# Stacked decoder blocks on one core: the expert weights of the second mixture dealt to the partitions in eights

## The reference, cut to what matters

```python
# t: 256 tokens x 1024 features; comb: 256 x 16 weights, non-zero in one group per token
a = silu(einsum('td,edf->tef', t, w_gate)) * einsum('td,edf->tef', t, w_up)   # w_gate, w_up: 16 x 1024 x 256
y = einsum('tef,efd->td', a * comb[:, :, None], w_down)                       # w_down: 16 x 256 x 1024
```

## Time and profile before

| what | us |
|---|---|
| median of 3 runs | 2881.32 |
| lowest and highest of them | 2875.06, 2892.28 |
| the profiled execution, its own time | 2874.71 |
| span of its instructions | 2872.9 |
| layer 0 of the second mixture, about | 2108 to 2298 |
| layer 1 of the second mixture, about | 2671 to 2853 |

### The profile page before, as it was taken

The page is one execution under the profiler, slowest core; times in us unless marked ns, Lnnn a source line. Parts: engine busy times, 40 slices in busy tenths (PEclk is TensorE's granted clock), DMA queues, the critical chain, the costliest instruction groups (busy, mean ns, idle before and its releaser), DMA issues. The chain is left out here.

```text
span 2872.9 us, 35384 instructions
## 1 busy us (share of the span) xinstructions
PE 2539.0 (88%) x15219; PEld 1502.3 (52%) x15219; DVE 794.5 (28%) x1806; ACT 410.5 (14%) x926; POOL 53.7 (2%) x67
## 2 busy tenths in 40 slices
PE   2889899998989999999997878689689977998997
PEld 2776788785773333333333323265554466656543
DVE  1211221288221122221212000124434413373122
ACT  1102000001121111011110000113211101352111
POOL 0000000070000000000000000000000000000000
PEclk9999999998989999999999999898879988697899
DMA  8333255642009999999999999932139962301481
GB/s 268 117 109 126 73 191 205 209 143 74 1 31 392 393 385 385 379 373 393 371 393 393 393 394 393 391 108 88 53 120 371 374 122 80 117 1 63 159 300 56
DMA packets 328586, 645.33 MB, mean 225 GB/s; under 512 B 12875, under 2 KB 98017, under 8 KB 328417
## 3 DMA queue, kind: packets, MB, share of 16 engines
q1 hardware_dynamic: 318608, 636.51, 61.4%
q10 hardware_dynamic: 9809, 6.41, 0.8%
HBM read 641.84 MB, written 1.05 MB: 224 GB/s over the span
## 5 line engine op out<-in xcount | busy, mean ns | idle before, releaser
L1330 PE MATMUL bank<-ring,xn 128*32 128x512 f32 x4896 | 564.3, 596 | 7.9 <-DMA ring<-od_moe_gu 6.2
L1142 PE MATMUL bank<-xn,ring 128*128 128x256 f32 x2048 | 462.9, 390 | 54.2 <-DVE xn L2878 17.7
L1142 PEld LDWEIGHTS bank<-xn,ring 128*128 128x128 f32 x2048 | 401.1, 196 | 116.6 <-issue 41.1
L1330 PEld LDWEIGHTS bank<-ring,xn 128*32 128x32 f32 x4896 | 157.1, 110 | 362.3 <-issue 349.0
L1395 PE MATMUL bank<-ring,att 128*32 128x512 f32 x2448 | 276.7, 593 | 1.3 <-ACT att L1961 1.3
L1295 PE MATMUL bank<-ring,xn 128*64 128x512 f32 x336 | 170.8, 658 | 64.9 <-issue 64.9
L2406 DVE TENSOR_TENSOR sq<-att,bank 32x512 f32<-32x512 f32 x70 | 48.0, 686 | 507.8 <-ACT att L1972 342.4
L1297 PE MATMUL bank<-ring,xn 128*64 128x512 f32 x336 | 171.2, 659 | 0.0
L1395 PEld LDWEIGHTS bank<-ring,att 128*32 128x32 f32 x2448 | 78.6, 110 | 171.9 <-issue 170.8
L1249 PE MATMUL bank<-xn,ring 128*128 128x256 f32 x704 | 153.6, 380 | 0.0
L1249 PEld LDWEIGHTS bank<-xn,ring 128*128 128x128 f32 x704 | 134.6, 191 | 18.7 <-issue 0.3
(11 more groups left out here) (265 smaller groups left out, 2324.0 us busy)
## 6 DMA issues: line engine op xcount, KB each, us to landing
ring<-od_moe_gu SPq DMA_DIRECT2D x112, 2048.0 KB, 17.3
ring<-od_moe_down SPq DMA_DIRECT2D x56, 2048.0 KB, 18.0
ring<-ada_w SPq DMA_DIRECT2D x24, 2048.0 KB, 15.1
ring<-moe_w_gate SPq DMA_DIRECT2D x32, 1024.0 KB, 9.2
ring<-moe_w_up SPq DMA_DIRECT2D x32, 1024.0 KB, 8.4
ring<-moe_w_down SPq DMA_DIRECT2D x16, 2048.0 KB, 13.8
ring<-ev_w_in SPq DMA_DIRECT2D x10, 2048.0 KB, 19.8
ring<-ev_ffn_gu SPq DMA_DIRECT2D x10, 2048.0 KB, 12.8
```

The costliest lines, as they stand in the source:

```text
L1142: mm = nc.tensor.matmul(ps[:, c * T:(c + 1) * T], kblk(b)[:, k, u * T + c * P:u * T + (c + 1) * P], x[:, k, :], start=k == 0, stop=k == KD ...
L1330: return nc.tensor.matmul(PSB[f.b][j * QP:(j + 1) * QP, :], src[:, k, at:at + QP], kblk(b)[:, k, :], start=k == 0, stop=k == KD - 1)
```

## The change

The 1024 feature rows of an expert's gate or up matrix are laid over the partitions in another way. Before, partition `p` got rows `p`, `p + 128`, `p + 256` and so on. Now it gets rows `8p` to `8p + 7`, which lie one behind the other in HBM, 8 KB in all. The place in SBUF is the same: eight pieces of 1 KB, 2 KB apart, because the two experts of a pair lie side by side in a slot. So that the tokens have their features in the same order, the gather for the second mixture takes as its stationary operand every eighth column of `xn_tok`, starting at `k`, in place of 128 neighbouring ones. The gather of the first mixture stays as it was. The number of loads, of matmuls and of all other instructions is unchanged. The load in the branch for more than 96 tokens and its gather are changed in the same way.

```diff
@@ experts
             def pair(W, n):
-                W = W[l].rearrange("e (k p) n -> e p k n", p=P)
+                W = W[l].rearrange("e (p k) n -> e p k n", p=P)
                 return [(lambda e, j: lambda b: (kblk(b)[:, :, j * E2_FF:(j + 1) * E2_FF], W[e]))(2 * n + j, j) for j in range(2)]
@@ SyncE, branch for groups over 96 tokens
-                                    src = W[st.l, g * EPG + 2 * n + j].rearrange("(k p) n -> p k n", p=P)
+                                    src = W[st.l, g * EPG + 2 * n + j].rearrange("(p k) n -> p k n", p=P)
@@ TensorE
-            def gather_pair(ps, i, w, take=gather):
+            def gather_pair(ps, i, w, take=gather, dealt=False):
                 for k in range(2 * i, 2 * i + 2):
                     for c in range(TC):
-                        mm = nc.tensor.matmul(ps[:, k % 2 * T:k % 2 * T + w], xn_tok[:, c, k * P:(k + 1) * P],
+                        features = slice(k, D, KD) if dealt else slice(k * P, (k + 1) * P)
+                        mm = nc.tensor.matmul(ps[:, k % 2 * T:k % 2 * T + w], xn_tok[:, c, features],
                                               take[:, c, 0:w], start=c == 0, stop=c == TC - 1)
                 return mm
-                        gather_pair(ps, i, GROUP_CAP, g_take[:, x]).then_inc(bank_full[f.b], 1)
+                        gather_pair(ps, i, GROUP_CAP, g_take[:, x], dealt=True).then_inc(bank_full[f.b], 1)
-                            mm = gather_pair(PSB[i], i, w, g_take_more)
+                            mm = gather_pair(PSB[i], i, w, g_take_more, dealt=True)
```

## The result

The changed kernel takes 2931.61 us (median of 4 runs, 2928.94 to 2931.96), the kernel before 2880.38 us beside it (4 runs, 2875.06 to 2892.28). The ratio is 1.0152, 95% interval [1.0118, 1.0185]; the two medians alone stand at 1.0178, inside it. It is slower by 1.5%, clear of the noise, as forecast, but the time lies 33 us above the forecast and 20 us above the range. Behind line 1412 every line number of the kernel after is one higher than before: the gather is line 1415.

The account below looks back on a forecast made before the run. TensorE was taken to bound the kernel, loads costing 0. Full-clock gathers +18.1, first gathers +1.0 and an absorbed wait -1.1 gave +18.0 us on 2881.3, so 2899 us; range 2877 to 2912, the forecast's own case 2894 to 2914.

Parts of the forecast that it names:

- The loads at 0: Second mixture's gate and up loads: new source pattern gains 0, since none of these loads ends a wait.
- Both rivals about them: Gate and up loads: slower, TensorE waits, 2895 us (chance 0.06); or faster, 2881 or up to some 10 less (0.04).
- the case that the 1 KB pieces cut the run up: Gate and up loads: destination pieces cut the 8 KB run; same 98017 packets under 2 KB, load time doesn't move.
- The shortest lead of 3.0 us: Layer 0, group 3: last gate load lands about 3.0 us before its matmuls begin, the cover if loads got slower.
- The rival that the weight load does not mind the step: Second mixture's gather: stepped columns cost 0, as do the loads, so the time is 2881 us; chance 0.32.
- The absorbed wait before the gather for group 1: Gather for group 1, both layers: a 0.56 us wait for VectorE hides part of the slowdown, -1.1 us.
- Second part: the gather: Second mixture's gather: weight load takes 205 ns a record at VectorE's price, 94 more; 192 full-clock records, +18.1 us.
- The bound above, twice the time of now: Second mixture's gather: a strided column takes twice the time at whatever clock, +32.3 us in all.
- The first gathers: First gather of each layer, at low clock: 189 ns a record becomes 205, 64 x 16 ns = +1.0 us.
- the bounds of +13.3 to +32.3: Gather's total cost: at least 75 ns a record more, at most twice the time per column; 2894 to 2914 us.
- The instructions behind the gather only move along: Instructions after the second mixture's gather: they start later, with no extra time of their own in the sum.
- The signs of the prediction: Profile after: gather of 32 records 6.6 us, a group 47.3 us in layer 0 and 45.1 in layer 1.

Follow-up runs that it names:

- e1: Kernel before with only the new source pattern of the gate and up loads, gather as before: 2894.65 us, ratio 1.0007.
- e3: Kernel before with the new loads, a contiguous gather, and features dealt earlier in ScalarE's four copies from PSUM: 2895.21 us, ratio 1.0016.
- e2: Kernel before with only the stepped gather (every eighth column), loads as before: 2931.56 us, ratio 1.0141.
- e4: Changed kernel with 192 moving columns in each gather matmul in place of 96, the second half unused: 2919.59 us, ratio 1.0094.
- e9: Kernel before with each gather matmul of the second mixture issued twice, both with neighbouring columns: 2910.66 us, ratio 1.0085.
- e5: Kernel before with line 1826 moving 120 columns in place of 60, the second 60 unused: 2872.73 us, ratio 0.9952.
- e6: Changed kernel with line 1826's matmuls moving 120 columns in place of 60: 2917.86 us, ratio 1.0105.
- e11: Changed kernel with 192 moving columns in the gather and 120 in line 1826's matmuls: 2905.88 us, ratio 1.0065.

## Why the prediction was right and where it was wrong

**What bounds the kernel: right.** TensorE did, a microsecond of the gather was a microsecond of the end, and no wait on a gate or up load appeared in any profile. (The prediction's "7.0 us in total" for the first mixture's weights is the row of the weight loads only; the matmuls' row of 6.2 us stands beside it. Neither is in the second mixture.)

**The loads at 0: right**, by the stages of e1, with the ratios of e1 (1.0007) and e3 (1.0016) beside them. Both rivals about them fall: they do not slow down, and they do not gain. The packets under 2 KB are unchanged, as the prediction had it for the case that the 1 KB pieces cut the run up. The shortest lead of 3.0 us was never needed.

**The mechanism of the gather: right.** The weight load paces it, the step lengthens the load, and nothing hides that. e2 shows that it is the whole of the loss. e4 bears out the pacing: twice the moving columns took no longer at full clock. The rival that the weight load does not mind the step, to which I gave 0.32, falls. The absorbed wait before the gather for group 1 is gone after, as said.

**The price of the step: too low.** The step that failed first is "Second part: the gather", 205 ns a record taken over from VectorE. Measured is 237 ns. For the 192 records that the sum has at full clock that is 126 ns more each and not 94: +22.8 us with the absorbed wait, in place of +17.0. The bound above, twice the time of now, was nearer. The step of the table is the better model: 16 bytes and more cost about double, 8 bytes next to nothing, and VectorE's 1.60 ns a number at 64 bytes was no measure of TensorE's 1.85 ns (237 / 128) at 32. That TensorE took 216 / 128 = 1.69 ns at 64 bytes is near VectorE's price, but one pair does not show a common limit.

**The first gathers: too low as well.** I took 205 ns as a limit of SBUF against the 189 of now and got +1.0 us. They went from 6.04 to 7.96 us, 249 ns a record, at a granted clock of 0.50: +3.7 us for both layers in place of +1.0. So the gathers cost 26.5 us and not 18.0, still within the bounds of +13.3 to +32.3. With this alone the time would have been 2908 and inside the range.

**The step that took the time out of the range: the clock, put at nothing, 12 us in the stages.** The sum moved line 1395 along at its 5.29 us, and line 1532 with it. In fact the gather with 96 columns in 237 ns lets the granted clock fall, and the matmuls behind it run partly or wholly at 1.2 GHz. e4 shows that it hangs on the columns that move: the same 237 ns with 192 of them keep 1.00, and all 12 us come back. e9 shows that it isn't the length. No bound of mine covered this; the prediction says "The instructions behind the gather only move along". With these 12 us on top of 2908 the time is 2920, above the 2912 of the range. The signs of the prediction show both steps: the gather takes 7.6 us and not 6.6, a group of layer 0 takes 49.1 and 50.2 us and not 47.3, and one of layer 1 47.4 and 47.6 and not 45.1.

**Outside the stages: some 12 us of the median that no step spoke of.** The medians differ by 51.2 us, the stages by 38.7. One part is line 1826, with 60 columns behind each weight load: it took 31.2, 42.3 or 57.0 us with what lies between its runs, and the profile that I read had it at its best. How often the kernel before has which is not shown, as it has one profile; e5 gained 9.9 us, and most of its times lie close together, but not all. The pair e5 and e6, where this stretch is at full clock in both, differs by 45.1, 7.1 more than their stages; e5 and e11 by 33.2, 5.0 more. By the profiles this last part sits in the attention of layer 1, which took 155.9 to 158.3 us in each of the seven profiles whose gather has a step of 16 bytes or more, and 140.9 to 152.9 in the six others. Neither its matmuls nor its loads are touched by the change. Where its time goes is the clock again: the granted clock of that stretch is 0.71 to 0.73 in the seven and 0.74 to 0.83 in the six. Why the clock is lower there stays open; no run here separates it.

## What to carry to other kernels

A matmul record whose stationary operand has its columns 16 bytes or more apart takes about twice the time of one with neighbouring columns (here, in float32 at full clock, 216 to 238 ns against 111), and where the weight load paces the matmuls, nothing hides it. If an order has to be changed, do it in a copy that is made anyway: ScalarE's copies with a read of PSUM at a step of eight took the same 565 to 587 ns. Matmuls that wait for their weight loads have columns to spare: moving more of them cost no time at full clock (1.1 us a gather at the lower one) and held the granted clock in the stages of e4. The same edit elsewhere made the one version that beats both kernels (e5, 0.9952 [0.9934, 0.997]). A stretch with few moving columns ran at either clock from one profile to the next, and one profile shows only one of them.

## What the runs showed of the hardware that was not expected

- The price of the step is a jump, not a slope: 111, 117, 232, 237 and 216 ns a record at 4, 8, 16, 32 and 64 bytes. The Trainium skill (SBUF — State Buffer, "Door 1: The DMA port swizzle") would have a float32 step of 4 numbers free; for TensorE's weight load the jump lies between 8 and 16 bytes, and the measurement decides. The same section of the Trainium skill asks for at least two accesses to a line of 16 bytes; by that a step of 2 numbers is free and one of 4 is not, and the trace agrees (117 and 232 ns).
- A stepped weight load hardly minds TensorE's clock: 32 records took 7.96 us at a granted clock of 0.50 and 7.62 at 1.00 (e4, third gather, 192 columns). Neighbouring columns did: 128 records of the same line took 27.30 us at 0.50 (e1) and 14.5 at 1.00 (before). So the step costs much less at the lower clock, 249 ns a record against 213. The weight loads alone say the same: a median of 337 ns for stepped ones at 0.50 (after, first gather) and of 338 at 1.00 (e4, third), 333 for neighbouring ones at 0.50 and 192 at 1.00. The first gather after, its weight loads, and those of line 1827 in e1:

```profile
2108.67:2116.63 7.96, 7.96 (x32) 7.72 (x32) 0.50 0.00 0
L1415 PEld LDWEIGHTS bank<-z,vtok x32: 312/337/337, 2108.6 to 2116.1; 128*128 128x128 f32 x32
L1827 PEld LDWEIGHTS bank<-memT,ring x128: 333/333/337, 2428.5 to 2455.8; 128*128 128x128 f32 x128
```

- TensorE counted as busy for the whole of a stretch is no sign that its clock stays up: 7.65 of 7.65 us busy at a granted clock of 0.80.
- A source run of 8 KB that lands in pieces of 1 KB left the packets (98017 under 2 KB) and the time as they were.
